# The first modulation of a DiT block kernel: where the scale vector is summed

## The reference, cut to what matters

```python
mod_l = (jax.nn.silu(c) @ w_ada[l] + b_ada[l]).reshape(B, N_MOD, 1, D)
mod_c = (jax.nn.silu(c_ctx) @ w_ada[l] + b_ada[l]).reshape(N_MOD, 1, 1, D)
...
def _modulate(x, shift, scale):
    return x * (1.0 + scale) + shift
...
    y = _swiglu(_modulate(x, shift, scale), w13, w2)
```

## Time and profile before

| | |
|---|---|
| median of 3 runs | 2127.93 us (2126.62 to 2128.96) |
| span of the profiled execution | 2127.8 us, 31643 instructions |
| TensorE busy | 2091.4 us (98%) |
| VectorE busy | 1527.0 us (72%) |
| ScalarE busy | 905.6 us (43%) |

### The profile page before, as it was taken

The page is one execution under the profiler, slowest core; times in us unless marked ns, Lnnn a source line. Parts: engine busy times, 40 slices in busy tenths (PEclk is TensorE's granted clock), DMA queues, the critical chain, the costliest instruction groups (busy, mean ns, idle before and its releaser), DMA issues.

```text
span 2127.8 us, 31643 instructions
## 1 busy us (share of the span) xinstructions
PE 2091.4 (98%) x11508; PEld 1768.0 (83%) x11510; DVE 1527.0 (72%) x2520; ACT 905.6 (43%) x1631; POOL 192.8 (9%) x212
## 2 busy tenths in 40 slices
PE   8999999999999999999999999999999999999998
PEld 4888888888888888899878878877888888888886
DVE  5778888777648878675665465866867777767787
ACT  4622222222237446542565555734532323336445
POOL 0000000000000001090111002821000000000001
PEclk9999999999999999999999999999999999999999
DMA  8144444555459664733231002732244434349773
GB/s 298 33 142 147 149 134 129 160 167 159 129 186 348 193 215 148 209 101 117 74 108 41 21 21 66 182 109 99 75 134 140 136 104 153 123 139 341 257 234 112
DMA packets 261841, 310.38 MB, mean 146 GB/s; under 512 B 19350, under 2 KB 164686, under 8 KB 261710
## 3 DMA queue, kind: packets, MB, share of 16 engines
q1 hardware_dynamic: 261422, 308.52, 45.4%
q10 hardware_dynamic: 288, 0.13, 0.0%
HBM read 242.13 MB, written 66.45 MB: 145 GB/s over the span
## 4 chain that ended last, share of the span: by engine, by line
PE 86%; DVE 4%; DMA 3%; ACT 2%; issue 1%; POOL 1%; SPq 1%; DVEq 0%; POOLq 0%; ACTq 0%
PE psum L1327 11%; PE psum L1328 11%; PE psum L1329 11%; PE psum L1527 6%; PE psum L1529 6%; PE psum L1528 6%; PE psum L2056 3%; PE psum L2058 3%; PE psum L2057 3%; PE psum L1347 2%; PE psum L1346 2%; PE psum L1345 2%; PE psum L3078 2%; PE psum L875 2%; PE psum L876 2%; PE psum L877 2%
## 5 line engine op out<-in xcount | busy, mean ns | idle before, releaser
L1327 PE MATMUL psum<-x_mix_h,x_op_h 128*128 128x512 f32 x640 | 251.2, 393 | 1.3 <-DVE v_sum L1135 1.2
L1328 PE MATMUL psum<-x_mix_l,x_op_h 128*128 128x512 f32 x640 | 249.8, 390 | 0.0
L1329 PE MATMUL psum<-x_mix_h,x_op_l 128*128 128x512 f32 x640 | 249.5, 390 | 0.0
L1527 PE MATMUL psum<-s_high 128*128 128x512 f32 x616 | 240.0, 390 | 0.3 <-DVE s_low L1514 0.3
L1528 PE MATMUL psum<-s_low,s_high 128*128 128x512 f32 x616 | 239.9, 389 | 0.0
L1529 PE MATMUL psum<-s_high,s_low 128*128 128x512 f32 x616 | 239.9, 389 | 0.0
L1514 DVE TENSOR_TENSOR s_low<-s_raw,s_high 128x1024 fp32r<-128x1024 f32 x154 | 186.9, 1217 | 50.5 <-ACT s_high L1475 50.5
L1475 ACT ACTIVATE s_high<-s_raw 128x1024 fp32r<-128x1024 f32 x154 | 161.3, 1057 | 124.1 <-PE psum L1529 56.3
L1019 ACT ACTIVATE x_op_h<-raw 128x512 fp32r<-128x512 f32 x140 | 86.1, 627 | 203.6 <-PE psum L1329 121.1
L1019 ACT ACTIVATE x_op_h<-w_sum 128x512 fp32r<-128x512 f32 x160 | 97.1, 625 | 162.9 <-DVE w_sum L997 107.1
L1327 PEld LDWEIGHTS psum<-x_mix_h,x_op_h 128*128 128x128 f32 x640 | 120.4, 188 | 25.4 <-issue 1.8
(11 more groups left out here) (408 smaller groups left out, 5069.6 us busy)
## 6 DMA issues: line engine op xcount, KB each, us to landing
raw<-in_ffn_w SPq DMA_DIRECT2D x88, 512.0 KB, 5.4
f_terms<-g_half SPq DMA_DIRECT2D x154, 256.0 KB, 2.3
s_raw<-f_terms SPq DMA_DIRECT2D x154, 256.0 KB, 3.2
s_raw<-in_ffn_w SPq DMA_DIRECT2D x154, 256.0 KB, 4.0
ada_slice<-in_w_ada SPq DMA_DIRECT2D x112, 256.0 KB, 3.1
c_raw<-in_ffn_w SPq DMA_DIRECT2D x22, 512.0 KB, 3.5
p_raw<-in_w_in SPq DMA_DIRECT2D x22, 512.0 KB, 4.0
early<-in_w_ada SPq DMA_DIRECT2D x16, 512.0 KB, 6.6
```

The source lines that it names most:

```text
L1327: nc.tensor.matmul(o, wh[:, k], high(k), start=i < 4 and k == 0, stop=False, skip_group_check=i > 3)
L1328: nc.tensor.matmul(o, wh[:, k], low(k), start=False, stop=False, skip_group_check=i > 3)
L1329: last = nc.tensor.matmul(o, wl[:, k], high(k), start=False, stop=k == KH - 1, skip_group_check=i > 3)
L1527: nc.tensor.matmul(o, h[:, 0, rows], h[:, 1], start=i == 0 and q in (0, 1, 6), stop=False, skip_group_check=True)
```

## The change

The scale vectors are summed as the shift vectors were: TensorE multiplies the slice of `more_c` with the scale tile, two products of 512 columns each, for K tiles 0 to 6. VectorE's sixteen passes and `early_sums` go; VectorE copies the scale row out of PSUM (`scale_row_dve`), ScalarE the shift row. The last K tile of both vectors is not summed as a row: each row is turned into columns by products with two rows of the identity, and the last tile's contribution is added into the same columns, by products with the tile as 128 x 128 weights and `more_c` as two columns (`last_columns_pe`). Both vectors (latent and context) come out at once, first for columns 0 and 1, then for 2 to 7. The four small loads are issued by ScalarE. The idle matmuls have other counts and another bank.

```diff
-        def early_scale_dve(dve, k):
-        def early_shift_pe(pe, k):
+        SHIFT_BANKS, SCALE_BANKS = (1, 7), (0, 2)
+        MOD_PARTS = ((0, 2), (2, KD))
+        KNOWN_ROWS = KD - 1
+
+        def early_rows_pe(pe, i, banks):
+
+            k = i // 2
+            wait_early(pe, i)
+            for half in range(2):
+                last = nc.tensor.matmul(psum[0:2, banks[half], :], more_c[:, k, :],
+                                        early[i][:, half * BANK:(half + 1) * BANK], start=k == 0, stop=k == KNOWN_ROWS - 1)
+            if k == KNOWN_ROWS - 1:
+                last.then_inc(row_summed_pe, 1)
...
-        def shift_turn_pe(pe):
-        def early_scale_pe(pe, v, parts):
-        def early_known_dve(dve, v, part):
+        def scale_row_dve(dve):
+
+            dve.wait_ge(row_summed_pe, ROWS_BEFORE + 2)
+            for half in range(2):
+                nc.vector.tensor_copy(scale_row[:, half * BANK:(half + 1) * BANK], psum[0:2, SCALE_BANKS[half], :])\
+                    .then_inc(scale_kept, 1)
+
+        def row_columns_pe(row, banks, part):
+
+            for n in range(*MOD_PARTS[part]):
+                nc.tensor.matmul(psum[:, banks[part], 2 * n:2 * n + 2], row[:, n * P:(n + 1) * P], ident[0:2, 0:2],
+                                 start=n == MOD_PARTS[part][0], stop=False, skip_group_check=True)
+
+        def last_columns_pe(i, banks, part):
+
+            for n in range(*MOD_PARTS[part]):
+                last = nc.tensor.matmul(psum[:, banks[part], 2 * n:2 * n + 2], early[i][:, n * P:(n + 1) * P],
+                                        more_c[:, KNOWN_ROWS, :], start=False, stop=True, skip_group_check=True)
+            return last
+
+        def early_columns_pe(pe):
+
+            pe.wait_ge(shift_kept, KEPT_BEFORE + 2)
+            for part in range(2):
+                row_columns_pe(shift_row, SHIFT_BANKS, part)
+            wait_early(pe, 2 * KNOWN_ROWS)
+            last_columns_pe(2 * KNOWN_ROWS, SHIFT_BANKS, 0)
+            pe.wait_ge(scale_kept, 2)
+            for part in range(2):
+                row_columns_pe(scale_row, SCALE_BANKS, part)
+            wait_early(pe, 2 * KNOWN_ROWS + 1)
+            last_columns_pe(2 * KNOWN_ROWS + 1, SCALE_BANKS, 0).then_inc(early_used, 1)
+            last_columns_pe(2 * KNOWN_ROWS, SHIFT_BANKS, 1)
+            last_columns_pe(2 * KNOWN_ROWS + 1, SCALE_BANKS, 1).then_inc(early_used, 1)
+
+        def early_known_dve(dve, part):
+            first, end = MOD_PARTS[part]
+            dve.wait_ge(early_used, part + 1)
+            for which, (to, banks) in enumerate(((in_scale, SCALE_BANKS), (in_shift, SHIFT_BANKS))):
+                nc.vector.tensor_tensor(to[:, :, first:end],
...
-            before, behind = (6, 2, 0, 0, 0, 0, 0, 0), (0, 0, 10, 0, 10, 3, 3, 2)
-            for k in range(KD):
+            before, behind = (3, 0, 0, 0, 0, 0, 0), (0, 0, 10, 1, 8, 1, 2)
+            for k in range(KNOWN_ROWS):
                 idle_pe(pe, before[k])
-                early_shift_pe(pe, k)
+                early_rows_pe(pe, 2 * k, SHIFT_BANKS)
                 if k == 1:
                     pe.wait_ge(bias_in, 3 * 16)
-                    nc.tensor.transpose(psum[:, 0, 0:120], rows_a[0:120, :], ident[0:120, 0:120]).then_inc(rows_turned, 1)
+                    nc.tensor.transpose(psum[:, 3, 0:120], rows_a[0:120, :], ident[0:120, 0:120]).then_inc(rows_turned, 1)
+                early_rows_pe(pe, 2 * k + 1, SCALE_BANKS)
+                if k == 3:
+                    pe.wait_ge(T1.scaled, KD)
                 idle_pe(pe, behind[k])
                 if k == 2:
+                    pe.wait_ge(rows_kept, 2)
                     turn_pe(pe, T1, T1_BANKS, rows_wait, 0)
-            early_scale_pe(pe, 0, (0,))
-            shift_turn_pe(pe)
-            early_scale_pe(pe, 0, (1,))
-            idle_pe(pe, 5)
+            early_columns_pe(pe)
+            idle_pe(pe, 2)
             pe.wait_ge(F1.lo, 2)
             pe.wait_ge(mod_ready, 2)
             for k in range(KD):
                 pe.wait_ge(T1.low, k + 1)
                 for part in range(2):
                     last = plain_step(pe, F1, 0, part, k)
-                if k == 0:
-                    early_scale_pe(pe, 1, (0, 1))
...
         def _(sp):
-            sp.dma_start(rows_b[0:8, :], c.rearrange("l (r p) -> (l r) p", p=P)).then_inc(rows_in, 16)
...
         def _(act):
+            act.dma_start(rows_b[0:8, :], c.rearrange("l (r p) -> (l r) p", p=P)).then_inc(rows_in, 16)
...
-                act.wait_ge(mod_ready, 1 + int(k >= SCALE_PARTS[1][0]))
+                act.wait_ge(mod_ready, 4 if k >= MOD_PARTS[1][0] else 2)
                 first_scaled_act(act, k)
...
-            for k in range(KD):
-                early_scale_dve(dve, k)
...
+            first_low(dve, F1)
+            scale_row_dve(dve)
+            early_known_dve(dve, 0)
             first_low_dve(dve, 0)
-            first_low_dve(dve, 1)
-            early_known_dve(dve, 1, 0)
-            early_known_dve(dve, 1, 1)
-            for k in range(2, KD):
+            early_known_dve(dve, 1)
+            for k in range(1, KD):
                 first_low_dve(dve, k)
```

More of the change, by code:

```diff
@@ L159, in hybrid_block @@
         early = [place(f"early{i}", 32 + 4 * i if i < 12 else 96 + 4 * i, [P, D]) for i in range(EARLY)]
-        early_sums = place("early_sums", 176, [P, 2, D])
+        scale_row = place("scale_row", 176, [2, D])
         early_bias = place("early_bias", 195, [P, 2, KD])
@@ L654, in wait_early @@
             engine.wait_ge(early_in[i % 4], 16 * (i // 4 + 1))
-        def early_scale_dve(dve, k):
[L658 to L666, removed]
-        def early_shift_pe(pe, k):
-            wait_early(pe, 2 * k)
-            for half in range(2):
[L672 to L677, removed]
+        SHIFT_BANKS, SCALE_BANKS = (1, 7), (0, 2)
[4 more added lines that the diff above has]
+            wait_early(pe, i)
+            for half in range(2):
+                last = nc.tensor.matmul(psum[0:2, banks[half], :], more_c[:, k, :],
+                                        early[i][:, half * BANK:(half + 1) * BANK], start=k == 0, stop=k == KNOWN_ROWS - 1)
+            if k == KNOWN_ROWS - 1:
+                last.then_inc(row_summed_pe, 1)
         def shift_row_act(act):
-            act.wait_ge(shift_summed, SUMMED_BEFORE + 1)
+            act.wait_ge(row_summed_pe, ROWS_BEFORE + 1)
             for half in range(2):
@@ new lines, in early_known_dve @@
+        def early_known_dve(dve, part):
[3 more added lines that the diff above has]
+                nc.vector.tensor_tensor(to[:, :, first:end],
+                                        psum[:, banks[part], 2 * first:2 * end].rearrange("p (k v) -> p v k", v=2),
+                                        early_bias[:, which, first:end].unsqueeze(1).to_broadcast([P, 2, end - first]),
+                                        ALU.add).then_inc(mod_ready, 1)
@@ L3673, in _ @@
             dve.wait_ge(rows_kept, 1)
[L3674 to L3683 removed]
+            dve.wait_ge(rows_turned, 2)
+            nc.vector.tensor_copy(params[:], psum[:, 3, 0:120]).then_inc(rows_kept, 1)
+            dve.wait_ge(rows_kept, 2)
+            nc.vector.tensor_scalar_add(early_bias[:, 0], params[:, KD:2 * KD], 1.0)
+            nc.vector.tensor_copy(early_bias[:, 1], params[:, 0:KD]).then_inc(rows_kept, 1)
             dve.wait_ge(rows_kept, 3)
[L3685 to L3686 removed]
+            first_low(dve, F1)
+            scale_row_dve(dve)
+            early_known_dve(dve, 0)
             first_low_dve(dve, 0)
[L3688 to L3691 removed]
+            early_known_dve(dve, 1)
+            for k in range(1, KD):
                 first_low_dve(dve, k)
```

14 lines of the change are left out of this document (7 added, 7 removed).

## The result

The changed kernel takes 2139.79 us (median of five runs, 2139.39 to 2144.16), the kernel before 2128.96 beside it (2126.62 to 2132.24): a ratio of 1.0054, 95% interval 1.0043 to 1.0064. So it is slower by 10.8 us, in the direction forecast and by more than forecast. The profiled spans are 2138.0 and 2127.8.

A forecast was written before the change was run, and what follows sets the result against it. TensorE's queue in the first 60 us was taken as the bound: +4.35 to the turning, +2.15 to F1's first product, -1.7 context products, +1.2 clock make +6.0 us on 2127.93, so 2133.9 us; range 2130.5 to 2137.5.

The forecast's parts named there:

- Rival 1: Start: TensorE keeps pace with tile landings at 1.15 us a tile; -3.5 us, 2124.4 us; chance 7 in 100.
- the sum: Start: TensorE's queue added up from 5.9 us, reaching the turning at 41.3, 4.35 us later than before.
- Silu came 1.06 after the fourth on SyncE (2.22 to 3.28), so it is at 4.55: ScalarE's start: Silu follows the last small load's issue by 1.06 us, 1.27 us late, so TensorE starts at 5.9.
- (a): SyncE's queue: four small loads leave it, so every tile lands 1.47 us sooner, the last at 34.1.
- The table load: ScalarE's start: taken to stay ahead of the four issues; behind them, Silu near 3.5 and TensorE at 4.85.
- the 6.0 of the sum: Start: time for the first three tiles, the first 2.5 us and each further tile 1.76 us.
- I take the row nearest in shape: Turning: two-row products priced like the eight two-row transposes, 0.073 us a record, 2.3 us for 32 records.
- half a price on it, 1.2: Turning: 3.2 us of thin products at low clock, cost between nothing and 2.3 us, taken half way.
- the upper bound that the prediction named: Turning: low clock costs thin products up to 2.3 us if their spacing follows it as the weight load does.
- a low clock past 52: F1's start: sign that would show the prediction wrong, TensorE's clock still low after 52 us.
- Rival 3: F1 or the start: a second low-clock stretch, +1.7 us; +7.7 us in all; chance 14 in 100.
- +8.8: Whole kernel: second low-clock stretch with thin work at its upper bound as well, 2136.7 us.

The follow-up runs named there:

- e1: Changed kernel with the four small loads back on SyncE's queue ahead of the tiles; ratio to the kernel before 1.0041.
- e2: Changed kernel without the 22 idle matmuls behind the tile products; ratio to the kernel before 1.0033.
- e3: Changed kernel without the products of the scale tiles of K tiles 0 to 5; ratio to the kernel before 1.0006.
- e5: Changed kernel with SyncE waiting for the four small loads, still issued by ScalarE, before its first tile; ratio to the kernel before 1.0042.
- e6: Changed kernel with the two rows turned by transposes instead of plain products; ratio to the kernel before 1.0040.
- e4: Kernel before with only its four small loads moved to ScalarE's queue; ratio to the kernel before 1.0000.
- e10: Kernel before with F1's first two weight loads behind the sixteenth tile, split by halves in the first two K steps; ratio 1.0015.
- e7: Changed kernel with nine more idle matmuls, in threes, among the turning's thin products; ratio to the kernel before 1.0063.
- e9: e8 with the last K tile also multiplied into the rows, its column products gone and eight idle matmuls behind the transposes; ratio to before 0.9998.
- e11: e10 with the 16 context products ahead of F1's first step in place of five idle matmuls; 2128.46 us, ratio to the kernel before 0.9990.
- e12: Kernel before with the 16 context products ahead of F1's first step in place of five idle matmuls; ratio to before 0.9998.
- e8: Changed kernel with small loads on SyncE, no idle matmuls behind tile products, and rows turned by transposes; ratio to before 1.0002.

## Why the prediction was right in its direction and short in its size

**Right: the mechanism.** TensorE's queue, from the copy of `more` to F1's first product, sets the start. After shows it without waits; e1, e2 and e3 take work or delay out of that queue at three places, and the turning moves by 4.7 (3.4 without the change of pace), 5.2 and 10.5 us. Rival 1 (TensorE keeps pace) asked for 1.15 us a tile; e3 gives 1.76. The middle of the queue, from the fourth tile to the turning, took 28.4 us (16.16 to 44.54) where the sum had 28.1.

**Wrong: the landing of the small loads.** The step that failed is "Silu came 1.06 after the fourth on SyncE (2.22 to 3.28), so it is at 4.55". Silu came at 7.14. The 1.06 is the price of a load that has the transfers to itself; moved to a second queue it runs beside the first 512 KB tiles and landed 5.08 after its issue. Alone, from the same queue, it had landed within 1.63 of it (e5). The one thing that (a) was to give, earlier landings, is what made it dear. The table load went the other way than chosen, behind the issues, and that did not matter, since it was over 3.47 before the last load. TensorE began 2.3 late, and the first three tiles, at the slower pace, took 0.6 longer than the 6.0 of the sum. How much of this 0.6 is the chance of one execution is not shown: the time at which the pace changes differs between executions that begin alike (last section).

**Wrong: the price of a row's products.** "I take the row nearest in shape", 0.073 a record, was mis-sized: 32 records took 3.74 instead of 2.3, 1.4 more. The nearest row was a transpose, and e6 shows that this, not the two rows of its weights, made it cheap. The Trainium skill (TensorE: Matmul & The Clock Gate, LDWEIGHTS) says that a weight load costs by its columns, and the prediction set that aside, though by that the rows would cost 1.1 of the 1.4; the plain products bear it out, by line after, in ns as least, median and most:

```profile
L687 PEld LDWEIGHTS psum<-ident,shift_row x16: 181/187/187, 44.5 to 46.2; 2*128 2x128 f32 x16
```

```profile
L693 PEld LDWEIGHTS psum<-more,early x32: 186/333/338, 46.4 to 53.6; 128*128 128x128 f32 x32
```

With 2 rows or 128 the least is alike, 181 and 186. The line of e6 for the transposes of the same 2 rows and 128 columns has another price, so there the trace does not agree:

```profile
L687 PEld LDWEIGHTS psum<-ident,shift_row x8: 134/136/138, 44.1 to 44.5; 2*128 2x128 f32 x8
```

**Mis-sized: the clock.** The prediction had the fall right in kind and half a price on it, 1.2. The spacing follows the clock (0.112 and 0.213): the 32 records of the last tiles took 5.6 us (0.54 and 5.07) instead of 3.35, 2.3 more, and 19 of them at the lower clock are 1.9 of it. That meets the upper bound that the prediction named, but by another course: the fall came 5.3 us after the first thin product (44.54 to 49.87), not 2.5 as before, and the low stretch was twice as long as before, so that "a low clock past 52", its own sign of being wrong, is there. Rival 3 had a second low stretch, at F1 or at the start. The first came, but lay mostly under the thin products, so that F1 lost 0.2 by it and not 1.7; of the second there is the 0.6 of the first three tiles. The result lies beyond its +8.8 all the same, since neither the late loads nor the rows are in it.

**The sum.** At F1's first Silu: 2.3 for the start, 0.1 for the idle matmuls, 0.6 for the first three tiles, 0.3 up to the turning, 1.4 for the rows, 1.1 for the clock beyond the 1.2, less 0.3 for idle matmuls that cost 0.45 and not 0.7, and 0.2 in F1: 5.7 on top of 6.0, and the profile has 11.65. By 2000 us the traces are 10.6 apart, with the 1.1 given back near 530 us and smaller shifts either way; the runs have 10.8. Why a program that starts later should not have the waits for `v_sum`, two of together 1.2, was not tested; that it has none is read from page part 5, before and after (line, busy and mean ns, idle and its releaser):

```profile
L1327 PE MATMUL psum<-x_mix_h,x_op_h 128*128 128x512 f32 x640 | 251.2, 393 | 1.3 <-DVE v_sum L1135 1.2
```

```profile
L1331 PE MATMUL psum<-x_mix_h,x_op_h 128*128 128x512 f32 x640 | 250.9, 392 | 0.2
```

The prediction counted on everything after F1 to shift whole; on the way the shift lay between 9.5 and 12.4.

## What to carry to other kernels

A transfer's price is that of the traffic it meets: before moving small loads to a queue of their own, look at what large transfers will then run beside them, and what they release (here Silu, `more` and TensorE's whole queue). When work moves to the engine whose queue sets the start, every tile counts in full (1.76 us here), and freeing VectorE bought nothing. A price taken from the nearest row holds for its operation too, not its shape alone: a transpose of two rows was 0.073 a record, a plain product of the same rows 0.117, twice.

## What the runs showed of the hardware

- TensorE's clock fell to 1.2 GHz with runs of thin products (one or two columns moved), though the engine reads as busy throughout. In e4 the fall came 1.1 us behind them, after four idle matmuls, and in e10 in TensorE's wait for F1's weights. Nine idle matmuls among the thin products did not hold it (e7); without such a run it did not fall at the start (e9). One fall had none ahead of it: in e11, in the transposes of x rows behind a wait of 2.27, where waits of 1.21 to 1.73 (before, e10, e12) brought none.
- How long the clock stays down was not foreseen: 3.4 us in before and e4, 6.8 in after, e8 and e11 (at F1), 10.2 in e1, e2, e3, e5, e6, e7 and e12, and 13.7 in e10, with TensorE partly waiting. What decides between these was not settled.
- The first tiles of after run at half pace under a granted clock that the windows give as full. A window, and two weight loads of its tile products:

```profile
10.00:12.00 2.00, 2.00 (x3) 0.26 (x2) 0.00 (x0) 0.00 (x0) 0.00 (x0) 1.00 1.04 416
```

```profile
10.39 0.13 PEld L665 LDWEIGHTS psum<-early,more 128*2 128x2 f32 x1 [0.72 <-issue]
11.24 0.13 PEld L665 LDWEIGHTS psum<-early,more 128*2 128x2 f32 x1 [0.72 <-issue]
```

They are 0.85 apart; later twelve records come in 5.31, 0.43 apart with the last one's tail counted once. The trace's records of the clock begin only where the pace changes, at 12.3 in after and 8.7 in before, and ahead of them the spacing of the records is to be trusted over that column. That point moves: 5.8, 8.8 and 10.7 in e1, e8 and e9, which begin alike, and 11.7 to 14.1 in the six kernels whose TensorE begins late (after, e2, e3, e4, e6, e7).
